# Transposes of later operand rounds behind the first matmuls, and two reorderings around the post-norm root

## The reference, cut to what matters

```python
def _half_ffn(x, g_pre, g_post, w_gate, w_up, w_down):
    h = _rmsnorm(x, g_pre)
    f = (jax.nn.silu(h @ w_gate) * (h @ w_up)) @ w_down
    return x + 0.5 * _rmsnorm(f, g_post)

def second_block(x, ...):
    for i in range(DEPTH):
        x = _half_ffn(x, ...)                       # f3, f5
        h = _rmsnorm(x, mix_norm_pre[i])
        m = _conformer_conv(h, ...) if i % N_MIXERS == 0 else _diff_attention(h, ...)
        x = x + _rmsnorm(m, mix_norm_post[i])
        x = _half_ffn(x, ...)                       # f4, f6
    return x
```

## Time and profile before

| | |
|---|---|
| median of three executions | 1887.2 us (1886.42 to 1892.06) |
| the profiled execution's own time | 1888.43 us |
| its span, first to last instruction | 1886.6 us |
| PE busy | 1729.1 us, 92% of the span |
| DVE busy | 1229.9 us, 65% |
| ACT busy | 817.3 us, 43% |
| mean granted TensorE clock | 0.96 of full speed |
| DMA | 285.93 MB, mean 152 GB/s |

### The profile page before, as it was taken

The page is one execution under the profiler, slowest core; times in us unless marked ns, Lnnn a source line. Parts: engine busy times, 40 slices in busy tenths (PEclk is TensorE's granted clock), DMA queues, the critical chain, the costliest instruction groups (busy, mean ns, idle before and its releaser), DMA issues.

```text
span 1886.6 us, 29289 instructions
## 1 busy us (share of the span) xinstructions
PE 1729.1 (92%) x11365; PEld 1591.6 (84%) x11365; DVE 1229.9 (65%) x1751; ACT 817.3 (43%) x1199; POOL 39.3 (2%) x23
## 2 busy tenths in 40 slices
PE   7869999997697999999989869999899989689998
PEld 7857799996577999999988769999899989479997
DVE  4778566666767566666668956565766554866665
ACT  4556444335344333534353054334533344754433
POOL 0000000000005000000000000000000000000000
PEclk9979999998798999999999989999999999889999
DMA  7610345453223545455434034545354545035544
GB/s 265 212 45 1 99 171 198 174 193 102 99 68 133 192 175 200 146 190 198 177 142 161 1 122 168 195 172 200 146 189 178 196 138 178 2 101 202 199 171 162
DMA packets 53291, 285.93 MB, mean 152 GB/s; under 512 B 5872, under 2 KB 6128, under 8 KB 30704
## 3 DMA queue, kind: packets, MB, share of 16 engines
q1 hardware_dynamic: 52224, 281.46, 41.5%
q0 software_dynamic: 1008, 3.67, 0.5%
HBM read 284.05 MB, written 1.05 MB: 151 GB/s over the span
## 4 chain that ended last, share of the span: by engine, by line
PE 82%; DVE 11%; ACT 4%; issue 2%; DMA 0%; DVEq 0%; SPq 0%; ACTq 0%
PE bank L827 18%; PE bank L828 17%; PE bank L829 17%; PE bank L987 9%; PE bank L956 3%; PE bank L958 3%; PE bank L960 3%; DVE proj L1743 3%; PE bank L841 2%; PE bank L1044 1%; PE bank L1003 1%; ACT whi L437 1%; PE bank L1024 1%; DVE nmax L1477 1%; DVE att L1475 1%
## 5 line engine op out<-in xcount | busy, mean ns | idle before, releaser
L827 PE MATMUL bank<-hthi,whi 128*128 128x256 f32 x2144 | 607.9, 284 | 1.9 <-DVE wlo L1274 1.8
L828 PE MATMUL bank<-htlo,whi 128*128 128x256 f32 x2144 | 607.2, 283 | 0.0
L829 PE MATMUL bank<-hthi,wlo 128*128 128x256 f32 x2144 | 607.1, 283 | 0.0
L1268 DVE TENSOR_TENSOR wlo<-raw,whi 128x2048 fp32r<-128x2048 f32 x175 | 401.4, 2294 | 97.5 <-ACT whi L437 97.3
L827 PEld LDWEIGHTS bank<-hthi,whi 128*128 128x128 f32 x2144 | 411.7, 192 | 7.3 <-DVE wlo L1274 2.2
L828 PEld LDWEIGHTS bank<-htlo,whi 128*128 128x128 f32 x2144 | 411.6, 192 | 4.7
L829 PEld LDWEIGHTS bank<-hthi,wlo 128*128 128x128 f32 x2144 | 411.6, 192 | 0.0
L437 ACT ACTIVATE whi<-raw 128x2048 fp32r<-128x2048 f32 x175 | 333.9, 1908 | 34.8 <-PE bank L829 27.3
L509 ACT ACTIVATE tr<-tr 128x256 f32<-128x256 f32 x132 | 55.1, 418 | 657.8 <-DVE tr L1352 657.8
L1352 DVE TENSOR_TENSOR tr<-bank,rb 128x512 f32<-128x512 f32 x132 | 91.2, 691 | 231.8 <-PE bank L829 231.6
L1274 DVE TENSOR_TENSOR wlo<-raw,whi 128x1024 fp32r<-128x1024 f32 x174 | 214.5, 1233 | 25.5 <-ACT whi L445 25.1
(11 more groups left out here) (241 smaller groups left out, 2088.9 us busy)
## 6 DMA issues: line engine op xcount, KB each, us to landing
raw<-in_stream SPq DMA_DIRECT2D x176, 1024.0 KB, 5.3
raw<-in_stream SPq DMA_DIRECT2D x176, 512.0 KB, 3.5
wide<-in_wide POOLq DMA_DIRECT2D x7, 512.0 KB, 4.1
x<-in_x SPq DMA_DIRECT2D x1, 1024.0 KB, 5.4
out<-x SPq DMA_DIRECT2D x2, 512.0 KB, 2.9
wide<-in_const SPq DMA_DIRECT2D x1, 960.0 KB, 15.5
const<-in_const SPq DMA_DIRECT2D x1, 897.0 KB, 12.7
cols<-in_cols SPq DMA_DIRECT2D x1, 340.0 KB, 7.8
```

Source lines behind the costliest of these rows:

```text
L827: nc.tensor.matmul(out, whi_, mhi, start=start, stop=False)
L828: nc.tensor.matmul(out, whi_, mlo, start=False, stop=False)
L829: return nc.tensor.matmul(out, wlo_, mhi, start=False, stop=stop)
L1268: V.tensor_tensor(wlo[:, s, 0:UA], raw[:, s, 0:UA], whi[:, s, 0:UA].bitcast(F32), ALU.subtract)\
```

## The change

Three edits. In `operand_ahead`, `ready(k)` before transposed round 2 ahead of chunk 0 and round 3 ahead of chunk 2, which waited for the banks of rounds 0 and 1 and so for these rounds' operands. Now chunks 0, 2, 4 and 6 wait for the operands of rounds 0 to 3, and the transposes of rounds 2 and 3 stand ahead of chunks 1 and 3. In ACT's stream `hi_a(U_F5 + 1)` stands behind `post_ffn(2)` where it stood ahead of it. In DVE's `post_ffn` the fourth `gained` stands behind the reciprocal: behind the first half's additions for k = 0, 2 and 3, and for k = 5, the end of the program, between the reciprocal and the additions.

```diff
@@ -786,8 +786,8 @@
             post_mixer(1)
             operand("op_f4", [(c, col("ffn_pre", 8 + c)) for c in range(DC)], U_F4)
             ffn(3, 6)
+            post_ffn(2, U_F4)
             hi_a(U_F5 + 1)
-            post_ffn(2, U_F4)
             operand("op_f5", [(c, col("ffn_pre", 16 + c)) for c in range(DC)], U_F5)
             ffn(4, 7)
             post_ffn(3, U_F5)
@@ -855,11 +855,11 @@
                     rounds(name, 1, P, lambda _: [(P, P, src(t, c)) for c in (2 * q, 2 * q + 1) for t in range(NT)], q)
 
                 def ready(k):
-                    if k % 2 == 0 and k < 4:
-                        one(k // 2 + 2)
-                    elif k % 2 == 0:
+                    if k % 2 == 0:
                         r = RD[name] + k // 2
                         pe.wait_ge(s_tf[r % 2], r // 2 + 1)
+                    elif k < 4:
+                        one(k // 2 + 2)
 
                 one(0)
                 one(1)
@@ -1393,11 +1393,12 @@
                 dve.wait_ge(s_pss, done + 4)
                 V.tensor_tensor(ss[:, 0:2], ss[:, 8:12].rearrange("p (t j) -> p t j", j=2)[:, :, 0],
                                 ss[:, 8:12].rearrange("p (t j) -> p t j", j=2)[:, :, 1], ALU.add).then_inc(s_phs, 1)
-                gained(3)
                 rstd(f"post{k}", 2)
                 if k < 5:
                     add_first_half(k)
+                    gained(3)
                     return
+                gained(3)
                 dve.wait_ge(s_fg, POST_BASE[k] + 4)
                 for j in range(2):
                     for t in range(NT):
```

## The result

| | before | after |
|---|---|---|
| median of the runs | 1886.8 us (1886.26 to 1892.06, 4 runs) | 1903.1 us (1901.39 to 1904.39, 4 runs) |
| profiled execution, own time | 1888.43 us | 1903.56 us |
| its span | 1886.6 us | 1901.8 us |
| mean granted TensorE clock | 0.96 | 0.955 |

After to before is 1.0085, with a 95% interval of 1.0071 to 1.0099. I had forecast 1890.5 us and a range up to 1894.5, so the result lies outside it.

The account below looks back on a forecast made before the run. TensorE was taken as the bound, 82% of the chain of waits. Lost 5.6, won 0 + 1.3 + 0.35 + 0.6 = 2.25: 3.3 us slower, so 1890.5 us, range 1885 to 1894.5.

Parts of the forecast that it names:

- The sum of stalls: In seven starts where x is there before round 0, round 3 comes one chunk later: 5.6 us lost.
- four stalls: Idle at chunk 5 of op_attn, op_kv, op_bq and op_wo of about 1.1, 1.4, 2.6 and 1.1 us, ended by `lo_b`.
- op_f2's 0.2: op_f2: later gate projection vanishes in the 9.01 us stall; VectorE's order against GpSimd may cost 0.2, between -2 and 0.8.
- The losses of op_attn and op_wo: Hardly any slack between round 3 and chunk 5: 1.1 us lost each, 2.2 together.
- Edits 2 and 3: Late `gained`: 0.25 us won each for k = 0, 2, 3, 0.4 lost at k = 5; moved `hi_a`: 0.58 gained.
- The post-norm starts: op_conv, op_f4, op_f5, op_qkv, op_f6: chunk 0 beside x's additions brings no gain (0.3 - 0.3); the clock brings 1.3.
- the clock returns earlier: op_f4, op_f5, op_f6, op_qkv: unbroken work starts about 1.5 us earlier, high clock may too; 1.3 taken, 3.0 at most.
- The stall before `gate_up` in op_f4: In op_f4 the filled wait for x turns up again as a stall of about 1.3 us before `gate_up`.
- the one on the clock: Clock term for post-norm starts: low level there, earlier return of the high one worth 1.3 us.
- a longer stall lowers the clock: Rival: longer chunk 5 stalls in op_bq, op_attn, op_kv, op_wo cause a slow stretch, 2.2 us; 1894.0 in all; chance 0.22.
- the 2.2 priced: Within the longer-stall rival: a slow stretch of 4.5 us like op_f5's doubles its matmuls' time, costing 2.2 us.
- The last sign of being wrong that I had named: Prediction is wrong if the clock's slow stretches change by more than 1 us each.

Follow-up runs that it names:

- x7: Kernel before with only the late fourth `gained` at all six post-norms and the moved `hi_a`, transposes not moved: 1888.2 us against 1887.0, ratio 1.0009.
- x4: Kernel before with five small VectorE operations ahead of `k_scaled()` as a mere delay, none of the edits: 1910.5 us against 1887.1, ratio 1.0122.
- x3: Changed kernel with 12 and 4 added, never read transposes in two waits ahead of the MLA attention: 1886.2 us against 1887.1 for before.
- x9: Kernel before with the delay of x4 and 16 unread transposes inside the MLA attention, behind the third head's scores: 1900.5 us, ratio to before 1.008.
- x5: Changed kernel run again, no edit: four executions of 1890.3 to 1890.7 us and four of 1900.9 to 1902.8, ratio 1.005.
- x2: Kernel before with the moved transposes only in op_attn, op_f1, op_kv and op_bq: 1893.1 us against 1887.1, ten executions, one of 1908.2.
- x13: Kernel before, no edits, with unread transposes added in TensorE's waits at post-norm starts, f2, the convolution and MLA projections: 1870.8 us against 1886.0, ratio 0.9918.
- x1: Change with moved transposes only in the five post-norm starts, late `gained` at all post-norms but the last, `hi_a` moved: 1884.4 us against 1887.1, ratio 0.9982.
- x14: Changed kernel with unread transposes added in TensorE's waits as in x13: 1878.0 us against 1886.0, ratio 0.9951.
- x6: Changed kernel with the same five small VectorE operations ahead of `k_scaled()` as in x4: 1909.1 us, ratio 1.0111.

## Why the prediction was wrong

- **The sum of stalls was right.** Round 3 a chunk later, and what stands behind it later one for one: four stalls within 0.1 us of the forecast. The losses were 0.75, 0.75, 0.9, 1.1, 0.3 and 0.8 for 5.6 forecast with op_f2's 0.2, 4.9 in all. The losses of op_attn and op_wo were oversized, 1.1 each: both stalled 1.05, and lost 0.75 and 0.3. In op_wo the level returned 6.4 us behind the start of round 0 instead of 8.2, which fits the part of its chunk that was not lost.
- **Edits 2 and 3 were right** in size (0.24 for 0.25, 0.59 for 0.6, and 0.5 lost at the end for 0.4), but by x7 they bring nothing measurable without edit 1 behind the post-norms.
- **The post-norm starts** gained 2.2 in the clock's and their own terms together for 1.3 forecast; "the clock returns earlier" holds in op_f5, where the low level lasted 3.4 us instead of 6.8, and hardly in op_f4 (back 8.3 us behind the start of round 0 instead of 8.5). The stall before `gate_up` in op_f4 was mis-sized, 0.44 for 1.3: a chunk that fills 1.42 us of a wait at 1.2 GHz leaves only 0.7 us open at 2.4 GHz where it stood.
- **The step that failed is the one on the clock.** It asked for the level only in "these five starts" and put its change at nothing, without a reason, everywhere else; the MLA attention stands in no term and in no rival, and there the runs show 16.3 us. The rival "a longer stall lowers the clock" did have half of the mechanism, and op_bq did it: these are the 4 us from chunk 5 on, before at 1.00 behind the stall of 1.51 us, after at 0.61 behind the one of 2.52.

```profile
449.30:453.30 4.00, 3.86 (x22) 1.00 0.42 137
```

```profile
452.30:456.30 4.00, 4.00 (x15) 0.61 0.49 139
```

- That cost 1.5 us, near the 2.2 priced. What I had not priced is a stretch in which the level, once low, does not come back: I took the length of a slow stretch from the earlier trace rows, 4.5 us, where the attention's is 37.5 (514.6 to 552.1). The last sign of being wrong that I had named, slow stretches that change by more than 1 us, is this one. The changed kernel arrives 3.3 us later at the attention: op_attn, op_f1, op_kv and op_bq lost 3.5 (3.7 forecast), and the first load and the level in between gave back 0.2. With that the fall and the return of the level lie otherwise against the transposes and the first score matmul. x4 shows that a delay can do it with none of the edits, x3 that the 17 us are gone with the level at 2.4 GHz, x9 that time comes back once the level is lifted inside the attention, x5 that it is open in each execution.
- The Trainium skill, "TensorE: Matmul & The Clock Gate", section "What's actually happening", says that the throttle's monitor runs freely of the kernel, so that the moment of a transition differs between runs. The two groups of x5 agree, 11 us apart. By the same section activity releases the throttle; in the changed kernel's attention 32 us of recorded activity without a gap (519.83 to 552.15) did not (x9: 13.8 us of scores not, 3.7 us of transposes yes).
- Open: why fp32 score matmuls at 1.2 GHz don't lift the level while at 2.4 GHz they hold it; what exactly tips an execution into the slow passage; and why the same code ahead of the attention did so in eight of twelve executions of the changed kernel and in one of ten of x2. Of the 75 executions of before, none did: they end at 1892.6, and none of those whose mean granted clock is on record is under 0.958.

## What to carry to other kernels

Ahead of each long dense stretch ask at which clock TensorE enters it, and price a shift by the longest stretch that would be run at 1.2 GHz, not by the nearest slow one. Fill TensorE's waits of 1 to 9 us with transposes that nobody reads, a little shorter than the wait: here that was worth 15 us (x13) on a kernel whose edits were worth 3 at best (x1). Where the wait got shorter, the same fill overran it and cost 1.5 us (x14). And run a changed kernel ten times before believing a median of four: it had two outcomes.

## What the hardware showed that I had not expected

- Once low, the level stayed at 0.50 for 37.5 us (after), 48 us (x4) and 55 us (x6). In after TensorE was busy without a gap from the first score at 519.83 on. Up to 538.2 it ran score matmuls alone; then groups of three transposes and the value matmuls came between them, and the level rose 14 us later.
- In the traces where the level did return in time it had fallen at 511.6, 515.2, 516.2, 515.3 and 515.6 us (before, x1, x2, x5, x7) and the scores began 4.4 to 4.9 us later; in x4, x9 and x6 they began 2.7 to 3.0 us later and it didn't. After is the exception: 5.2 us, and it didn't either. There the queries' transposes began 0.4 us behind the fall, in the first five between 0.2 ahead of it and 0.3 behind.
- In op_f2 of the changed kernel, the low part of a weight piece that takes VectorE 2.28 us elsewhere took 4.26 beside GpSimd's multiplies (591.2 to 615.2 us), the next one 4.04 for 1.23, and a copy with one input (L1358, 128x256) 4.69 for 0.29:

```profile
599.76 4.26 DVE L1268 TENSOR_TENSOR wlo<-raw,whi 128x2048 fp32r<-128x2048 f32 x1
...
604.13 4.04 DVE L1274 TENSOR_TENSOR wlo<-raw,whi 128x1024 fp32r<-128x1024 f32 x1
```
